# Latent attention queries of a two-block transformer kernel: plain columns projected already turned, rotated columns through tokens

## The reference

```python
def mla_mixer(c_q, c_kv, k_rope_raw, pos, q_norm, w_uq, kv_norm, w_ukv):
    q = (rmsnorm(c_q, q_norm) @ w_uq).reshape(b, s, 8, 64 + 32)
    q_nope, q_rope = q[..., :64], rope(q[..., 64:], pos)
    kv = (rmsnorm(c_kv, kv_norm) @ w_ukv).reshape(b, s, 8, 64 + 64)
    k_nope, v = kv[..., :64], kv[..., 64:]
    k_rope = rope(k_rope_raw[:, :, None, :], pos)[:, :, 0]
    # by blocks of 128 queries:
    sc = einsum('bqhd,bkhd->bhqk', qn, k_nope) + einsum('bqhd,bkd->bhqk', qr, k_rope)
    p = softmax(where(causal, sc * 96 ** -0.5, -1e30))
    o = einsum('bhqk,bkhd->bqhd', p, v)
```

## Time and profile before

| | |
|---|---|
| median of three runs | 2040.94 us |
| profiled execution, its own time | 2040.94 us |
| its span, first to last instruction | 2039.1 us |
| granted TensorE clock, mean | 0.999 |
| PE busy | 2031.1 us (100%) |
| DVE busy | 1388.8 us (68%) |
| ACT busy | 1018.9 us (50%) |
| POOL busy | 92.6 us (5%) |

### The profile page before, as it was taken

One profiled execution on the slowest core, in us unless ns is written; L12 is line 12 of the kernel. 1 busy time (PEld: TensorE's weight loads), 2 busy tenths in 40 slices (PEclk: granted clock), 3 DMA queues, 4 the chain that ended last, 5 costly groups with the idle time before them and its releaser, 6 DMA issues.

```text
span 2039.1 us, 25100 instructions
## 1 busy us (share of the span) xinstructions
PE 2031.1 (100%) x10332; PEld 1714.0 (84%) x10332; DVE 1388.8 (68%) x1626; ACT 1018.9 (50%) x1290; POOL 92.6 (5%) x133
## 2 busy tenths in 40 slices
PE   9999999999999999999999999999999999999998
PEld 7888888888888888888888888888888888888887
DVE  6655687775757566877675667757767677577675
ACT  6444576453445335775443365644444466445331
POOL 1001010000010001100100000000100000000000
PEclk9999999999999999999999999999999999999999
DMA  9655544565566656544656474555655656455552
GB/s 333 211 187 167 183 162 140 166 213 186 187 198 210 193 170 201 166 145 145 226 190 197 152 245 152 169 174 172 239 187 190 203 154 198 153 186 195 195 189 83
DMA packets 225569, 377.73 MB, mean 185 GB/s; under 512 B 6592, under 2 KB 113216, under 8 KB 225456
## 3 DMA queue, kind: packets, MB, share of 16 engines
q1 hardware_dynamic: 221472, 362.64, 54.1%
q0 software_dynamic: 3984, 13.49, 2.2%
HBM read 375.05 MB, written 1.05 MB: 184 GB/s over the span
## 4 chain that ended last, share of the span: by engine, by line
PE 98%; DVE 1%; ACT 0%; issue 0%; DVEq 0%; POOL 0%; ACTq 0%; POOLq 0%
PE pb L1663 64%; PE pb L1674 18%; PE pb L1677 9%; PE pb L1686 2%; PE pb L1732 1%; PE pb L1810 1%; DVE wl L2117 0%; PE pb L1809 0%; PE pb L1797 0%; PE pb L1865 0%; PE pb L1789 0%; PE pb L1652 0%; DVE lS L2300 0%; PE pb L1656 0%; PE pb L1691 0%; PE pb L1654 0%
## 5 line engine op out<-in xcount | busy, mean ns | idle before, releaser
L1896 ACT ACTIVATE wh<-raw 128x2048 fp32r<-128x2048 f32 (+2 forms) x347 | 654.3, 1886 | 626.3 <-PE pb L1663 267.0
L2117 DVE TENSOR_TENSOR wl<-raw,wh 128x2048 fp32r<-128x2048 f32 (+2 forms) x345 | 774.7, 2252 | 149.2 <-ACT wh L1896 148.3
L1663 PE MATMUL pb<-wh,x 128*128 128x512 f32 (+1 forms) x2144 | 651.1, 385 | 0.0
L1663 PEld LDWEIGHTS pb<-wh,x 128*128 128x128 f32 x2144 | 400.6, 188 | 77.9
L1663 PE MATMUL pb<-wl,x 128*128 128x512 f32 (+1 forms) x1072 | 421.1, 393 | 0.1
L1674 PE MATMUL pb<-x,wh 128*128 128x512 f32 x1568 | 397.0, 395 | 0.0
L1674 PEld LDWEIGHTS pb<-x,wh 128*128 128x128 f32 x1568 | 283.3, 189 | 51.8
L1663 PE MATMUL pb<-wl,mh 128*128 128x512 f32 (+1 forms) x740 | 255.7, 391 | 0.0
L1663 PE MATMUL pb<-wh,ml 128*128 128x512 f32 (+1 forms) x740 | 253.7, 388 | 0.0
L1663 PE MATMUL pb<-wh,mh 128*128 128x512 f32 (+1 forms) x740 | 253.4, 388 | 0.0
L1663 PEld LDWEIGHTS pb<-wl,x 128*128 128x128 f32 x1072 | 201.4, 188 | 42.2 <-issue 3.7
(11 more groups left out here) (363 smaller groups left out, 1595.8 us busy)
## 6 DMA issues: line engine op xcount, KB each, us to landing
raw<-in_w_in_dram SPq DMA_DIRECT2D x100, 1024.0 KB, 5.3
raw<-in_w_ff_dram SPq DMA_DIRECT2D x64, 1024.0 KB, 5.2
raw<-in_ffn_w_down_dram SPq DMA_DIRECT2D x44, 1024.0 KB, 4.9
raw<-in_ffn_w_up_dram SPq DMA_DIRECT2D x42, 1024.0 KB, 5.4
raw<-in_ffn_w_gate_dram SPq DMA_DIRECT2D x41, 1024.0 KB, 5.3
raw<-in_w_branch_dram SPq DMA_DIRECT2D x24, 1024.0 KB, 5.0
raw<-in_w_out_dram SPq DMA_DIRECT2D x16, 1024.0 KB, 5.0
raw<-in_w_in_dram SPq DMA_DIRECT2D x4, 832.0 KB, 4.5
```

What stands on the lines that cost most here:

```text
L1663: ins = e.matmul(pb[b][:, 0:c1 - c0], x[:, s, cols], w[:, n, c0:c1], start=(it["first"] and n == 0 and q == 0), stop=(it["stop"] and n == ...
L1896: e.activation(hi, raw, ACT.Copy).then_inc(m.high_done, 1)
L2117: e.tensor_tensor(lo, raw, hi.bitcast(F32), ALU.subtract).then_inc(m.low_done, 1)
```

## The change

- `mla_w_uq` is reordered on the host: first the 512 plain columns of all heads, then the 256 rotated ones.
- `latent_q` takes the place of the group. It lists two `qpart` products (one for each token half, 6 matmuls of 256 columns each, into side banks), ACT's copies to the new tile `qr` (`qsave`, without the wait for `kr_turned`), and POOL's rotation, then a tick; then twice a `qnope` product (12 matmuls of 256 columns with the weights as the stationary operand, into bank 0 and bank 2), its two copies to `qT` (even heads by ACT after `kr_turned`, odd heads by DVE after ACT), and a tick. So there are three ticks in the place of two.
- `mla_lane` transposes the rotated columns of all heads at once (`qrturn`, 4 transposes), and DVE places them in `qT` in four copies (`qplace`). `mla_pair` has no transposes and no copies of queries of its own, and its scores come at once, one tick earlier in each pair; `pscore` reads `qT`.
- The rope's scratch moves within `xn`; `yT` lies over `qT`, and its halves become contiguous.
- The constants `scan` and `chunk` share their memory with a buffer of the softmax (`lS30`), and both are loaded together ahead of the last feed-forward of the first block; the second block's scan and masks wait for both.

```diff
+        self.scan = A("scan", o_sc, [P, S])
+        self.chunk = A("chunk", o_sc + 1024, [P, P], U32)
...
-        o_q = rt(6144)
-        self.q = A("q", o_q, [P, 2, 8, 96])
+        o_q = rt(8192)
+        self.qT = A("qT", o_q, [P, 8, S])
+        self.qr = A("qr", o_lane[2], [P, 2, 8, 32])
         self.cn = A("cn", o_q, [P, 2, 384])
         o_kt = rt(8192)
...
-        self.rope_tmp = A("rope_tmp", o_xn, [P, 512])
+        self.rope_tmp = A("rope_tmp", o_xn + 6144, [P, 512])
...
@@ -1015,16 +1015,12 @@
             self.lane_free[i] = ("evac", w)
             done.append(w)
 
-    def mla_pair(self, f, done):
-
-        use = self.side()
-        v = self.pe("qturn2", f=f, use=use, need=self.qk)
-        self.add("qcopy2", use=use, p=v["p"], free=[self.lane_free[2], self.lane_free[3]])
-        yield
-        got, n, c = use, [], []
+    def mla_pair(self, l, f, placed, done):
+
+        got, n, c = ("evac", placed) if f % 2 else ("q_placed", l + 1), [], []
         for i in (2, 3):
             w, h = self.side(), 2 * f + i - 2
-            v = self.pe("pscore", kind="mla", i=i, h=h, use=w, need=[("evac", got)] + self.qk)
+            v = self.pe("pscore", kind="mla", i=i, h=h, use=w, need=[got] + self.qk)
             n.append(self.exps(i, 0, "plain", 96 ** -0.5, h, w, v["p"]))
         for i in (2, 3):
             c.append(self.next("weights"))
@@ -1151,21 +1147,18 @@
             self.pump()
         self.add("krrope", n=l, need=[self.ready["C", 2, 0], self.ready["C", 2, 1]])
 
-        q_toks = []
-
-        def q_epi(t, p, uses):
-            for b in range(2):
-                self.add("qsave", t=t, b=b, p=p, use=uses[b], n=l)
...
-        self.latent_kv(l, q_toks)
+        self.latent_q(l)
+        self.latent_kv(l)
 
         def mla_lane():
             yield
             yield
...
+            v = self.pe("qrturn", use=use, need=[("q_turned", l + 1)])
+            self.add("qplace", use=use, p=v["p"])
+            yield
             for f in range(4):
-                yield from self.mla_pair(f, mla_done)
+                yield from self.mla_pair(l, f, use, mla_done)
 
         def diff_end():
             while len(diff_done) < 8:
@@ -1215,7 +1208,27 @@
         for s in range(8):
             self.m_free[s] = self.np - 1
 
-    def latent_kv(self, l, q_toks):
+    def latent_q(self, l):
+        j = self.take(("mla_w_uq", (l,), 0, 2, 0, 768))
+        self.split(j)
+        need, toks, self.qk = self.need("C", [0, 1], [0, 1]), [], []
+        for t in range(2):
+            use = self.side()
+            v = self.pe("qpart", j=j, t=t, use=use, need=need)
+            self.add("qsave", t=t, p=v["p"], use=use)
+            toks.append(("evac", use))
+        self.add("qrope", n=l, need=toks)
+        self.tick()
+        for i in range(2):
+            use = self.use(2 * i)
+            v = self.pe("qnope", j=j, i=i, use=use)
+            self.add("qnsave", i=i, p=v["p"], use=use, n=l)
+            self.qk.append(("evac", use))
+            if i:
+                self.freed[j] = v["p"]
+            self.tick()
+
...
+    def latent_kv(self, l):
         j = self.take(("mla_w_ukv", (l,), 0, 1, 0, 1024))
         self.split(j)
...
-        self.add("qrope", n=l, need=q_toks, p=pk[1])
         self.kv = [("evac", sides[0]), ("evac", sides[1])]
-        self.qk = [("q_turned", l + 1), ("kr_saved", l + 1)]
+        self.qk += [("evac", uses[0]), ("evac", uses[1]), ("kr_saved", l + 1)]
         self.flush()
         self.advance()
 
...
+
+    def loads_between(self):
+        self.loads2(0)
+        self.add("chunk")
 
...
             po.all_ready(it["need"])
-            rope(po, e, m, 0, m.q, 8, 64, m.rope_tmp, m.q_turned)
+            rope(po, e, m, 0, m.qr, 8, 0, m.rope_tmp, m.q_turned)
...
-        elif k == "qturn2":
-            bank, f = pb[use[0]], it["f"]
+        elif k == "qpart":
+            hi, lo = [w[:, :, 512:768] for w in m.weights(it["j"])]
+            bank, c = pb[use[0]][:, 0:256], slice(t * P, t * P + P)
+            pe.wait_ge(m.low_done, it["j"] + 1)
             pe.all_ready(it["need"])
             pe.wait_ge(m.evac[use[0]], use[1])
+            for s in range(2):
+                e.matmul(bank, m.ch[:, s, c], lo[:, s, :], start=(s == 0), stop=False)
+                e.matmul(bank, m.ch[:, s, c], hi[:, s, :], start=False, stop=False)
+                ins = e.matmul(bank, m.cl[:, s, c], hi[:, s, :], start=False, stop=(s == 1))
+            ins.then_inc(m.pe_done, 1)
+        elif k == "qnope":
+            hi, lo = m.weights(it["j"])
+            pe.wait_ge(m.evac[use[0]], use[1])
             for q in range(2):
+                o, c = pb[use[0]][:, q * S:q * S + S], slice((2 * i + q) * P, (2 * i + q) * P + P)
+                for s in range(2):
+                    e.matmul(o, lo[:, s, c], m.ch[:, s, :], start=(s == 0), stop=False, skip_group_check=True)
+                    e.matmul(o, hi[:, s, c], m.ch[:, s, :], start=False, stop=False, skip_group_check=True)
+                    ins = e.matmul(o, hi[:, s, c], m.cl[:, s, :], start=False, stop=(s == 1), skip_group_check=True)
...
+        elif k == "qrturn":
+            bank = pb[use[0]]
+            pe.all_ready(it["need"])
+            pe.wait_ge(m.evac[use[0]], use[1])
+            for g in range(2):
...
                 for c in range(2):
-                    o = S * q + P * c
-                    ins = e.transpose(bank[0:96, o:o + P], m.q[:, c, 2 * f + q, :], ident[:, :])
+                    o = S * g + P * c
+                    ins = e.transpose(bank[:, o:o + P], m.qr[:, c, 4 * g:4 * g + 4, :].rearrange("p h n -> p (h n)"),
+                                      ident[:, :])
             ins.then_inc(m.pe_done, 1)
...
-            w, key = (96, m.kT[0:96, it["h"], :]) if it["kind"] == "mla" else (128, Q[:, 256:512])
+            bank, h = pb[use[0]], it["h"]
+            if it["kind"] == "mla":
+                query, key = m.qT[0:96, h, :], m.kT[0:96, h, :]
+            else:
+                query, key = m.lQ[i][:, 0:S], m.lQ[i][:, S:2 * S]
             pe.all_ready(it["need"])
             pe.wait_ge(m.evac[use[0]], use[1])
-            e.matmul(bank[:, 0:128], Q[0:w, 0:P], key[:, 0:128], start=True, stop=True)
-            e.matmul(bank[:, 128:384], Q[0:w, P:S], key, start=True, stop=True).then_inc(m.pe_done, 1)
+            e.matmul(bank[:, 0:128], query[:, 0:P], key[:, 0:128], start=True, stop=True)
+            e.matmul(bank[:, 128:384], query[:, P:S], key, start=True, stop=True).then_inc(m.pe_done, 1)
...
         elif k == "qsave":
-            b = it["b"]
+            a.pe(p)
+            e.activation(m.qr[:, t, :, :].rearrange("p h n -> p (h n)"), bank[:, 0:256],
+                         ACT.Copy).then_inc(m.evac[use[0]], 1)
+        elif k == "qnsave":
             a.pe(p)
             a.wait_ge(m.kr_turned, n + 1)
-            e.activation(m.q[:, t, 4 * b:4 * b + 4, :], bank[:, 0:384].rearrange("p (h n) -> p h n", n=96),
-                         ACT.Copy).then_inc(m.evac[use[0]], 1)
+            e.activation(m.qT[0:64, 4 * i:4 * i + 4:2, :], bank[0:64, :].rearrange("p (a s) -> p a s", s=S),
+                         ACT.Copy).then_inc(m.q_even, 1)
...
-        elif k == "qcopy2":
-            a.pe(p)
-            a.all_ready(it["free"])
-            e.activation(m.lQ[2][0:96, 0:S], bank[0:96, 0:S], ACT.Copy)
-            e.activation(m.lQ[3][0:96, 0:S], bank[0:96, S:2 * S], ACT.Copy).then_inc(m.evac[use[0]], 1)
...
         elif k == "ycopy":
             a.pe(p)
-            e.activation(m.yT[:, :, it["f"], 0:P], bank[:, 0:S].rearrange("p (t n) -> p t n", n=P),
-                         ACT.Copy).then_inc(m.evac[use[0]], 1)
+            e.activation(m.yT[:, it["f"], :], bank[:, 0:S], ACT.Copy).then_inc(m.evac[use[0]], 1)
...
+        elif k == "qnsave":
+            v.wait_ge(m.q_even, 2 * n + i + 1)
+            e.tensor_copy(m.qT[0:64, 4 * i + 1:4 * i + 4:2, :],
+                          bank[64:P, :].rearrange("p (a s) -> p a s", s=S)).then_inc(m.evac[use[0]], 1)
+        elif k == "qplace":
+            v.pe(p)
+            for r in range(4):
+                ins = e.tensor_copy(m.qT[64:96, r:8:4, :], bank[32 * r:32 * r + 32, :].rearrange("p (g s) -> p g s", s=S))
+                if r == 1:
+                    ins.then_inc(m.q_placed, 1)
+            ins.then_inc(m.evac[use[0]], 1)
```

More of the change, by code:

```diff
@@ L105, in __init__ @@
         self.kr_turned, self.q_turned = s("kr_turned"), s("q_turned")
-        self.kr_half = s("kr_half")
+        self.q_even, self.q_placed = s("q_even"), s("q_placed")
         self.weights_ready, self.y_high, self.y_low = s("weights_ready"), s("y_high"), s("y_low")
@@ L128, in __init__ @@
                       "recip_ready": self.recip_ready, "gla_keys": self.gla_keys, "gla_rstd": self.gla_rstd,
-                      "gla_done": self.gla_done, "q_turned": self.q_turned,
+                      "gla_done": self.gla_done, "q_turned": self.q_turned, "q_placed": self.q_placed,
```

(33 more changed lines are left out.)

16 lines of the change are left out of this document (5 added, 11 removed).

## The result

The changed kernel takes 2054.1 us (2053.93 to 2055.61, 5 runs), the kernel before beside it 2041.1 us (2040.9 to 2041.45, 5 runs): ratio 1.0065, 95% interval 1.0054 to 1.0077. It is slower, by 13.0 us; 2051.0 was forecast, within 2042 to 2057.

What follows compares the result with a forecast made beforehand. PE, busy 2031.1 of 2039.1 us, was taken as the bound. New waits of 3.1 + 3.05 + 1.2 = 7.35 us less 2.1 gave +5.2 a layer, +10.5 on 2040.94: 2051.4, said as 2051; range 2042 to 2057.

Steps and rivals of the forecast that it cites:

- PE's own work: PE's instructions and old waits around the latent queries: without any new wait a layer gains 2.1 us (0.5 + 1.2 + 0.4).
- the first term: Two old PE waits, before the first 384-column matmul and at the second head's `weigh`, go: gain 0.5 us a layer.
- the other two: Four `qturn2` go and one `qrturn` comes, 1.2 us; later pairs' scores follow `weigh2` in the same tick, 0.4.
- First new wait: Third tick: PE at second `dscore` waits 1.05 us for ACT's `wcopy`; with the following side-bank waits 3.1 us a layer.
- Rival 3: POOL's query rotation beside DVE's key rotation delays `qnsave` and all behind by up to 2.2 us a layer; 2055.8; chance 0.18.
- `kvv`, `kvv`, `krturn`: Behind the early `dscore`, PE waits for DVE to free three maps' side banks: 0.8 + 0.5 + 0.7 us a layer.
- Second new wait: Next pair's scores: PE at the third `dscore` waits 3.05 us a layer for `wcopy`, behind late latent additions and a `high`.
- Third: The same pattern once more at the last `dscore`: PE waits 1.2 us a layer.
- Rival 1: Only the first wait is real; ACT and DVE absorb the second and third; 2042.9 us; chance 0.18.
- Rival 2: No new wait, since `wcopy` and the additions come in time; 2036.7 us, faster by 0.2%; chance 0.09.
- Rival 4: The change doesn't do what it says, the transposes return elsewhere; given no chance.

Runs made afterwards that it cites:

- experiment 1: Kernel before with only a third tick between query projection and `latent_kv`: 2056.01 us; repeated with the keys' bank need at the scores alone: 2056.2 us.
- experiment 2: Changed kernel without the tick behind the second `qnope`, so two ticks, placing copies still on DVE: 2048.24 us, ratio 1.0035 to the kernel before.
- experiment 4: Changed kernel with its three ticks, only the four placing copies moved from DVE to ACT: 2050.02 us, ratio 1.0042 to the kernel before.
- experiment 5: Changed kernel with POOL's rotation of the queries listed behind `latent_kv`, as before the change: 2056.44 us, ratio 1.0077 to the kernel before.
- experiment 7: Changed kernel with 8 and 12 unused 512-column matmuls ahead of the second and third `dscore`: 2053.38 us, ratio 1.0059 to the kernel before.
- experiment 6: Changed kernel with the latent lane started one tick later: 2051.17 us, ratio 1.0048 to the kernel before.
- third tick alone in its second version: Kernel before with only a third tick, the need for the keys' two copies on the scores, not the query transposes: 2056.2 us, ratio 1.0073.
- experiment 3 with DVE: Changed kernel with two ticks, `qrturn` and `qplace` two ticks earlier, placing copies still on DVE: 2043.48 us, ratio 1.0014 to the kernel before.

## Why the prediction was right, and where not

The sign, the range and the mechanism held: PE is the bound, and new waits of PE outweigh a small gain in its own work. By its steps, a layer (first layer / second):

- **PE's own work**, forecast -2.1 us. With no new wait the span is 3.2 us under that of before, 1.6 a layer. So the gain was counted 0.5 too large. 256-column steps take 0.119 us as taken, and the first term, 0.5, came out: from the transpose to the gates' first matmul that kernel takes 9.32 us (251.63 to 260.95), against 9.86. What is short lies in the other two, `qturn2` and the joins of the later pairs (forecast 1.6, left for them 1.1), which were not measured apart.
- **First new wait, `dscore`**, forecast 1.05, measured 1.84 / 1.85. The mechanism is right (experiments 1, 2 and 4). Mis-sized, because DVE's rotation was given as undisturbed and POOL as the one that gives way; experiment 5 gives 0.99. Rival 3 had this mechanism, at up to 2.2 us a layer; it is worth 0.85 at this wait. That its time, 2055.8, is nearer to the measured one than the forecast's is chance, since most of the difference is the clock.
- **`kvv`, `kvv`, `krturn`**, forecast 0.8 + 0.5 + 0.7, measured 0.86 + 0.28 + 0.44 in the second layer, and 0.86 alone in the first, where the slow clock covered the rest.
- **Second new wait**, forecast 3.05, measured 2.58 / 3.01; experiment 4 shows that DVE's placing copies make it: with them on ACT it is 0.24.
- **Third**, forecast 1.2, measured 0.23 / 0.23. The chain was counted on over 22 us with every item at its full price; that was too far.
- **Not in the forecast**: the clock, 3.4 / 1.7 us, which experiment 7 shows to follow from the standstills. Every wait was priced at its own length. The three falls are 5.1 us of the 14.1. A term for it was missing, and that is the largest error of the sum.

Sum of the terms, measured: waits 5.5 / 6.7, clock 3.4 / 1.7, own work -1.6 / -1.6: +7.3 and +6.8, together 14.1; forecast were 5.2 and 5.2. So the forecast was low by the clock and POOL's hold, and high by the third wait, with the rest about even. That the total is within 3.1 us owes something to luck: errors of 5.1 and 1.6 us on the one side were met by 1.9 for the third wait and 1.6 at `kvv` and `krturn` on the other.

Rival 1 (only the first wait) falls, since the second wait is there at nearly full size. Rival 2 (no new wait, 2036.7) is what the kernel with two ticks and ACT's copies reaches, at 2037.5: the projection is worth 0.17% where nothing waits for it. Rival 4 falls: the trace has four transposes of queries a layer, those of `qrturn`.

## What to carry to other kernels

When one engine is the bound, price an edit to the order of work by what the next consumer of each bank meets, and then ask what that standstill costs behind itself. Small copies that feed the bound belong on the engine whose queue is short at that moment, whichever does the neighbouring work: the same four copies on DVE cost 10.7 us more than on ACT with two ticks (2048.24 against 2037.5) and 4.1 more with three (2054.1 against 2050.02). ACT starts them 0.8 us after the transposes that feed them, and with two ticks PE never waits for them. And a wait taken away by moving work may come back one consumer later, as in experiments 5 and 6, so look at the whole list of waits, not at the one removed.

## What the runs showed of the hardware

- **The clock behind a standstill.** After PE had stood still for 1.6 to 3.4 us, the granted clock was 0.50 (1.2 GHz in place of 2.4) for some time, although PE was busy again at once. Each fall cost one of two sizes: 1.7 us (changed kernel at 262 and 289, two ticks at 280) or 3.4 (third tick alone in its second version, both layers; one layer in experiments 4 and 6). It did not follow every such wait: 1.84 us at 260.15 in experiment 4 cost no clock, 1.85 us at 849.56 in the same run 3.4 us. Waits of up to 1.2 us cost none in the profiled execution of experiment 3 with DVE; its other executions may differ, as said there. What decides between the cases is open. The Trainium skill ("TensorE: Matmul & The Clock Gate", section "HAM oscillation — how this bites in real kernels") describes pauses of the matmuls that bring the clock down and have to be paid for anew each time; the trace agrees in that, with 5.1 us over three pauses. But by the page's rule most pauses of this length would have been harmless, and here the measurement decides. With 5.1 us more the forecast of 2051.4 would have been 2056.5, nearer to the profiled execution's 2055.04.
- **DVE and POOL hold each other up** in both directions: 32-element instructions of DVE of 0.18 us took 0.60 beside POOL, DVE's combination of 0.48 took 1.03 (experiment 5), and POOL's of 0.73 took 2.86 beside a DVE instruction of 2.28. Which of the two is held does not follow from the listed starts.
- **Copies of 512 columns out of the accumulation banks took the same on 32 as on 64 partitions**: 0.70 us each on DVE; 0.60 and 0.59 on ACT.
